# A hybrid decoder step: earlier conditioning weights, convolution taps by channel block, and eight weight slots for the experts

## The reference, cut to what matters

```python
def ada_mod(c, w, b):                       # 9 conditioning rows, w is 1024 x 6144 per layer
    return jnp.split(jax.nn.silu(c) @ w + b, 6, axis=-1)

# layer 0: attention beside a Conformer convolution
q, k, v, ga, gb = jnp.split(h @ w_in, ...)  # 5 blocks of 512 columns
q = rmsnorm(q, q_gain); k = rmsnorm(k, k_gain)           # by heads of 64
u = ga * jax.nn.sigmoid(gb)
cv, new_buf = causal_dwconv(u, conv_buf, cb_w)           # 31 taps, 512 channels
cv = jax.nn.silu(layernorm(cv + cb_b, cb_ln_g, cb_ln_b))
out = jnp.concatenate([o, cv], axis=-1) @ w_out

# layer 1: a short gated convolution; after each: a mixture of 32 experts
g_idx = argmax(xf @ w_group + b_group)                   # 1 of 4 groups
top_v, top_i = lax.top_k(e_in_group, 2)                  # 2 of its 8 experts
y_e = (jax.nn.silu(x @ gate[e]) * (x @ up[e])) @ down[e] # 1024 -> 2*512 -> 1024
```

## Time and profile before

| what | value |
|---|---|
| runs of the kernel before (three) | 2438.08, 2447.42, 2448.91 us; median 2447.42 |
| the profiled execution | 2444.9 us, its span 2443.2 us |
| PE busy | 1804.6 us (74%) in matmuls |
| DVE, ACT, POOL busy | 487.0, 300.4, 179.7 us |
| data moved | 604.27 MB, mean 247 GB/s |
| granted TensorE clock, mean | 0.863 of full speed |

### The profile page before, as it was taken

One profiled execution on the slowest core, in us unless ns is written; L12 is line 12 of the kernel. 1 busy time (PEld: TensorE's weight loads), 2 busy tenths in 40 slices (PEclk: granted clock), 3 DMA queues, 4 the chain that ended last, 5 costly groups with the idle time before them and its releaser, 6 DMA issues. The chain is left out here.

```text
span 2443.2 us, 26085 instructions
## 1 busy us (share of the span) xinstructions
PE 1804.6 (74%) x8637; PEld 846.2 (35%) x8638; DVE 487.0 (20%) x989; ACT 300.4 (12%) x563; POOL 179.7 (7%) x167
## 2 busy tenths in 40 slices
PE   3779877368867478888888718999944788787682
PEld 1335333134433333333333204555442333332231
DVE  0010695332132201100000031121131010000003
ACT  1130111322101010010101012000020101010001
POOL 0000111001102200000000030000121000000004
PEclk8769989568688589999999968999967999899896
DMA  7992203907701277799999990010045999999994
GB/s 252 387 383 72 69 18 104 351 30 238 285 22 69 91 301 272 297 407 410 408 411 411 410 342 2 1 69 2 35 172 215 354 366 411 409 411 411 411 410 174
DMA packets 194115, 604.27 MB, mean 247 GB/s; under 512 B 15951, under 2 KB 18288, under 8 KB 193897
## 3 DMA queue, kind: packets, MB, share of 16 engines
q1 hardware_dynamic: 158064, 522.21, 55.1%
q10 hardware_dynamic: 25761, 46.50, 5.2%
q0 software_dynamic: 10208, 34.48, 4.0%
HBM read 551.57 MB, written 52.01 MB: 247 GB/s over the span
## 5 line engine op out<-in xcount | busy, mean ns | idle before, releaser
L780 PE MATMUL ps<-ring,W 128*64 128x512 f32 x2048 | 465.4, 605 | 55.5 <-issue 32.7
L793 PE MATMUL ps<-ring,W 128*64 128x512 f32 x1024 | 272.8, 680 | 52.0 <-DVE W L1591 47.2
L780 PEld LDWEIGHTS ps<-ring,W 128*64 128x64 f32 x2048 | 173.2, 139 | 335.7 <-issue 334.9
L909 ACT ACTIVATE W<-ps 128x512 f32<-128x512 f32 (+4 forms) x243 | 134.5, 568 | 973.5 <-PE ps L793 364.3
L1585 DVE TENSOR_TENSOR W<-W,ps 128x256 f32<-128x256 f32 x64 | 26.9, 421 | 796.4 <-ACT W L1175 796.4
L886 PE MATMUL ps<-hT,ring 128*128 128x512 f32 x384 | 170.7, 597 | 0.5 <-DVE W L1609 0.5
L793 PEld LDWEIGHTS ps<-ring,W 128*64 128x64 f32 x1024 | 91.0, 155 | 193.3 <-issue 193.3
L545 PE MATMUL ps<-ring,hT 128*128 128x512 f32 (+1 forms) x240 | 116.9, 646 | 1.9 <-DVE W L1292 1.9
L467 PE MATMUL ps<-ring,cT 128*32 128x512 f32 x384 | 75.8, 931 | 31.9 <-DMA ring<-in_w_ada_dram 31.7
L886 PEld LDWEIGHTS ps<-hT,ring 128*128 128x128 f32 x384 | 71.1, 190 | 80.9 <-issue 80.4
L1304 DVE SCALAR_TENSOR_TENSOR W<-W,prm 128x512 f32<-128x512 f32 x120 | 89.5, 817 | 0.0
(11 more groups left out here) (280 smaller groups left out, 1553.4 us busy)
## 6 DMA issues: line engine op xcount, KB each, us to landing
ring<-in_w_gate_up_dram SPq DMA_DIRECT2D x128, 2048.0 KB, 16.8
ring<-in_w_down_dram SPq DMA_DIRECT2D x64, 2048.0 KB, 17.0
ring<-in_w_ada_dram SPq DMA_DIRECT2D x24, 2048.0 KB, 19.7
x_rows<-X ACTq DMA_DIRECT2D x1, 18944.0 KB, 53.0
ring<-in_cache_k_dram SPq DMA_DIRECT2D x64, 256.0 KB, 3.0
W<-x_rows SPq DMA_DIRECT2D x32, 512.0 KB, 17.8
x_rows<-W ACTq DMA_DIRECT2D x128, 128.0 KB, 5.9
ring<-in_cache_v_dram POOLq DMA_DIRECT2D x48, 256.0 KB, 4.6
```

The lines of the kernel that those rows point to most:

```text
L780: x = mm(ps[CAP * z:CAP * z + CAP, 2 + j, :], xt[:, k, :], at[:, :, 256 * z:256 * z + 256], start=(k == 0), stop=(k == KD - 1))
L793: x = mm(ps[CAP * z:CAP * z + CAP, 5 + j, :], ht[:, k % 2, CAP * (k // 2):CAP * (k // 2) + CAP], ring[:, 3 * j + 2, at:at + 512], start=(k ...
L909: return fn(out, src, ACT.Copy, **k)
```

## The change

Three parts are made together.

1. **Start.** PE adds to `slot_free` as its first act. ACT's transfers get semaphores of their own: `c_in` (c and the constants), `params_in` (nine), `misc_in` (gains of q and k, lambda). ACT computes `silu(c)` after three transfers, and issues `x_prompt` behind that. The eight router transfers move from ACT's queue to SP's, behind the first slot of `w_out_a`.
2. **Convolution.** Taps run by channel block, one block after the other: even taps sum in `cv`, odd taps in the block of `V` not yet in use, and one addition joins them (128 steps in all). 18 steps stand behind each of the first three u steps, and 8 in each q or k turn. ACT waits for the last steps before it writes `V`. The state's load goes to the `raw` area.
3. **Experts.** The ring gets slots 6 and 7, which are `Hb` and `hT` when the router has used them. The 96 loads of a layer go round the eight slots in order, so that a load waits for the part eight loads before. `each_expert` is one loop of four turns over eight experts. A pair of rows beyond the last is fetched and turned too (17 pairs instead of 16), and further passes' rows start 128 later.

```diff
-PAIRS = E // 2
+PAIRS = E // 2 + 1
+NRING = 8
+LOADS = 3 * E // NRING
+        slots = [ring[:, s, :] for s in range(NSLOT)] + [hflat[:, 0:SLOT], tflat[:, 0:SLOT]]
+        steps = [(c, k) for c in range(4) for k in range(BW + 1)]
+        WITH_U, WITH_QK = 18, 8
         def each_expert(eng, step):
-...
+            with eng.Fori(0, E // 8) as r:
+                for i in range(8):
+                    p, q = 4 * r + i // 2, i // 2 + 1
+                    step(8 * r + i, i, r, p, i // 2 % 2, (q % 2, 2 * r + q // 2, 4 * r + q) if i % 2 else None)
+        def place(i, k):
+            return divmod(3 * i + k, NRING)
...
@@ sync
+            for l in range(2):
+                for dst, src in ((rb[:, l, 0:G], a["b_group"][l:l + 1, :].to_broadcast([P, G])),
...
+                    sp.dma_start(dst, src).then_inc(S["route_in"], 16)
...
+                def fetch(r, i, parts=(0, 1, 2)):
+                    for k in parts:
+                        before, part_before = divmod(3 * i + k - NRING, 3)
+                        sp.wait_ge(M[("g0_mm", "gu_mm", "down_mm")[part_before]], done(l, 8 * r + before))
+                        part(EG * (i % 4) + 2 * r + i // 4, k, place(i, k)[1])
+                        if k == 1 and i % 2 == 0:
+                            rows_in(4 * r + (i // 2 + 1), (i // 2 + 1) % 2)
                 layer_wait(sp, l, "disp", 32 * NT)
                 rows_in(0, 0)
                 rows_in(1, 1)
+                layer_wait(sp, l, "lg_mm", 1)
+                part(2 * EG, 0, 6)
+                part(2 * EG, 1, 7)
+                rows_in(2, 0)
+                fetch(0, 2, (2,))
+                for i in range(3, 8):
+                    fetch(0, i)
+                with sp.Fori(1, E // 8) as r:
+                    for i in range(8):
+                        fetch(r, i)
@@ tensor
+            for s in range(NSLOT):
+                pe.sem_inc(slot_free[s], 1)
...
-            pe.wait_ge(S["params_in"], 16 * 26)
+            pe.wait_ge(S["c_in"], 48)
@@ scalar
+            act.wait_ge(S["c_in"], 48)
+            fn(W[0:9, W_C:W_C + D], W[0:9, W_C:W_C + D], ACT.Silu).then_inc(S["c_ev"], 1)
 ...
...
+                if u == 2 * NT:
+                    act.wait_ge(S["conv"], conv_done(2, BW))
@@ vector
+            def conv_step(n):
+                c, k = steps[n]
+                if k == 0:
+                    dve.wait_ge(S["u_ok"], 2 * c + 2)
+                to = V[:, c if c < 3 else LS, :] if k % 2 else cv[:, c, 0:TP]
+                if k >= 2:
+                    dve.wait_ge(S["conv"], n - (1 if k < BW else 0))
...
+                if m < 3:
+                    for n in range(WITH_U * m, WITH_U * (m + 1)):
+                        conv_step(n)
...
-                for n in range(per * u, min(per * u + per, 4 * BW)):
-                    conv_tap(n)
+                for n in range(3 * WITH_U + WITH_QK * u, min(3 * WITH_U + WITH_QK * (u + 1), len(steps))):
+                    conv_step(n)
```

More of the change, by code:

```diff
@@ L213, in mod @@
             return modT[:, MODS * KD * l + KD * m:MODS * KD * l + KD * m + KD, :]
-        slot_in = [sem(f"slot_in{s}") for s in range(NSLOT)]
+        slot_in = [sem(f"slot_in{s}") for s in range(NRING)]
         v_in = [sem(f"v_in{j}") for j in range(2)]
@@ L357, in experts, with part @@
                 dn = a["w_down"][l].rearrange("e (k p) n -> e p k n", p=P)
[L359 removed]
+                def part(e, k, s):
                     src = gu[e, :, 4 * k:4 * k + 4, :] if k < 2 else dn[e, :, :, :]
[L361 to L362 removed]
+                    sp.dma_start(slots[s].rearrange("p (k n) -> p k n", k=4), src).then_inc(slot_in[s], 16)
                 for s in range(NSLOT):
@@ L392, in experts @@
                 rows_in(1, 1)
[L393 to L409, removed]
+                layer_wait(sp, l, "lg_mm", 1)
[8 more added lines that the diff above has]
+                        fetch(r, i)
             experts(0)
             winc = a["w_in_c"][0].rearrange("(k p) n -> p k n", p=P)
-            for j in range(2):
-                for k in slots_done(0, E - 2 + j):
-                    col = D * k + 512 * j
-                    load(3 * j + k, winc[:, :, col:col + 512])
+            for s in range(NSLOT):
+                last, part_last = divmod(3 * E - NRING + s, 3)
+                sp.wait_ge(M[("g0_mm", "gu_mm", "down_mm")[part_last]], done(0, last))
+                col = D * (s % 3) + 512 * (s // 3)
+                load(s, winc[:, :, col:col + 512])
             woutc = a["w_out_c"][0].rearrange("(k p) n -> p k n", p=P)
@@ L457, in _ @@
             pe.sem_inc(S["row_tr"], 2)
-            for s in range(NSLOT):
-                pe.sem_inc(slot_free[s], 1)
+            pe.wait_ge(S["params_in"], 16 * 9)
+            tr(ps[:, 6, 0:96], W[0:96, 0:P], ident[0:96, 0:96])
+            tr(ps[:, 6, 96:165], W[0:69, P:2 * P], ident[0:69, 0:69])
+            tr(ps[:, 6, 165:289], W[0:124, 2 * P:3 * P], ident[0:124, 0:124]).then_inc(S["prm_tr"], 1)
             with pe.Fori(0, 4) as it:
@@ L774, in ffn, with gate_up @@
                 layer_wait(pe, l, "gate2_ev", 4)
-                def gate_up(xt, j, half, signal):
+                def gate_up(xt, i, half, signal):
+                    j, slot = i % 2, slots[place(i, half)[1]]
                     for k in range(4 * half, 4 * half + 4):
-                        at = ring[:, 3 * j + half, D * (k % 4):D * (k % 4) + D].rearrange("p (g f) -> p g f", g=2)
+                        at = slot[:, D * (k % 4):D * (k % 4) + D].rearrange("p (g f) -> p g f", g=2)
                         for z in range(2):
@@ L787, in h_turns, with down @@
                     x.then_inc(signal, 1)
-                def down(ht, j, signal):
+                def down(ht, i, signal):
+                    j, slot = i % 2, slots[place(i, 2)[1]]
                     for k in range(FE // P):
@@ L837, in one_pass @@
                                 x = mm(ps[XC * z:XC * z + XC, 5 + j, 0:256], hhT2[:, k, :],
-                                       ring[:, 3 * j + 2, at:at + 256], start=(k == 0), stop=(k == 3))
+                                       slots[place(i, 2)[1]][:, at:at + 256], start=(k == 0), stop=(k == 3))
                         x.then_inc(F["products"], 1)
```

167 lines of the change are left out of this document (78 added, 89 removed).

## The result

The changed kernel takes **2487.2 us** (median of 4, 2477 to 2509) where the kernel before takes 2446.6: the ratio is 1.018, with a 95% interval of 1.011 to 1.026. It is slower; forecast were 2417 us. The profiled execution took 2494.8 us with a span of 2493.0, 49.8 us more than the span of before, 2443.2.

A forecast was written before the change was run, and what follows sets the result against it. Transfers were taken to bound the start, DVE's taps the convolution, and PE, with loop code fetched anew, the experts. 2444.9 - 19 - 33 + 24 = 2417 us, range 2372 to 2446.

The forecast's parts named there:

- Part 1: Start, `w_ada` stage: first weight load at about 1 us instead of 28.38, gain 19 us, bounds 12 and 27.
- ACT's late entry: Start: ACT enters its loop near 28 us, behind the lambda transfers, at little cost; at 35 us in the lower bound.
- Part 2: Taps' stage: a turn on DVE falls from 11.52 to 7.8 us, nine intervals, gain 33 us.
- The rival by which the two-deep chain waits for itself: Taps on DVE: steps cost 0.9 us, a turn 9.0, gain only 22, total 2428 us; no chance of its own given.
- Part 3: Experts: more PE time for new loop code outweighs the ring's lead; layer 0 +18, layer 1 +6, together +24 us.
- the price of the code of the loop: Experts' loop: twelve packets do not stay; nine more misses at 4.1 us, 37 us of PE per layer.
- the price of a table load: Experts, ACT's silu table: 2.9 us per load, three fewer loads give back 9 us per layer.
- the third load ahead: Experts' start, a sign: SP issues three weight loads between rows and first freed slot; the working said two loads ahead.
- The mean price of an ordinary late step: Experts, PE on new code: mean idle 2.85 us per late step, besides +1.3 for the dearer product.
- a sign of a slower kernel: Experts: more than one step in three starting late would mean slower; about one in four was expected.
- The upper bound of +57: Experts, part 3's upper bound: 5.5 us a miss and no table load saved, 45 us per layer.
- The slower rival: Experts: a miss at every branch over the passes' code, +220 us, 2613 us; over 2460 us had chance 0.08.

The follow-up runs named there:

- experiment 1: The changed start and taps on the kernel before, with its experts (six slots, loop of four steps) untouched: 2396.9 us, ratio 0.981.
- Experiment 8: The changed kernel with PE's 32 expert steps written out and the other engines' loops untouched: 2437.5 us, ratio 0.995 to the kernel before.
- experiment 4: The changed kernel with six slots, four steps in the loop and 93 never-executed PE products added per step: 2817.7 us, ratio 1.152 to the kernel before.
- experiments 3 to 7 and 12: Changed kernel with six slots: eight steps (2489.1 us), or four steps plus 93, 24, 38, 54, 12 never-executed products per step (2817.7, 2635, 2715, 2714, 2433 and 2484).

## Why the prediction was wrong

- **Part 1: right.** Forecast were 19 us from a load at 1 us; the norm's transposes, which follow the stage, start at 158.04 instead of 176.80, 18.8 us. ACT's late entry came at 33.5 us, in the bounds given, and cost nothing, since the transfers and not PE set the stage's end.
- **Part 2: right.** Forecast 33 us, measured 31.3 (50.1 us ahead at 360.83, less 18.8). The turn is 8.1 us for 7.8. The rival by which the two-deep chain waits for itself, 0.9 us a step, fell: eight steps take 6.39 us, 0.80 each, though that is a little over the 0.747 of the forecast.
- **Between them and the experts** 3.5 us were lost. Profiled executions of nearly the same code take 444.0 us (experiment 1), 450.7 (before) and 454.2 (changed) from the barrier behind the taps to the first gate-up product, so I give this no cause.
- **Part 3: the step that failed**, the price of the code of the loop. Right were that twelve packets do not stay, that the passes' code and not the ring matters, that PE would wait for no weight (12 us given back in layer 0 and 26 in layer 1; forecast 10 and 22), and that silu's table is loaded eight times. Wrong was the price of a table load, 2.9 us: PE's waits for DVE shrank by 3 and 5.5 us per layer, forecast 9. The two steps compared, 15.86 and 12.92 us, differ in more than the load: the second turns a pair of rows, during which silu is made, and its down products take 3.65 us where the first's take 5.35. The next step of the first's kind without a load, 2040.74 to 2055.21 in the trace of before, takes 14.47 us, which makes 1.4 us a load and 4 for three. Also wrong, but of no weight, was the third load ahead: there are two, as the working itself said.

The sum of part 3 was to be +24 us and is +56.9 and +42.4, 99 us. Its terms in layer 0, forecast against measured (the measured ones over 815 to 1431 of the changed kernel and 861 to 1421 of the kernel before; PE was busy for 454.17 us there):

| term, layer 0 | forecast | measured |
|---|---|---|
| three branches back, pause | 3 x 2.85 = 8.6 | 29.6 |
| other late steps, pause, less those of before | 6 x 2.85 = 17 | 30.3 - 7.2 = 23.1 |
| products dearer (lower granted clock) | 9 x 1.3 = 12 | 472.37 - 454.17 = 18.2 |
| fewer table loads (waits for DVE) | -9 | -3 |
| waits for weights given back | -10 | -12 |
| sum | +18 | +56 |

Of the 18.2 us, 1.1 are the turn of the added pair of rows. PE's waits for DVE of all kinds were 73.3 us before and are 70.5; the largest part, ahead of the turns of h, in us, number and longest, before and after:

```profile
PE ps L786 <- DVE W L1585: 29.9, 24, 2.5
```

```profile
PE ps L797 <- DVE W L1613: 24.3, 20, 2.5
```

The mean price of an ordinary late step was right: 30.3 / 10 = 3.0 us for 2.85. There were more of them (ten, not eight; thirteen in layer 1); with the branches back 13 and 16 of 32 steps came late, over one in three, which the prediction had named as a sign of a slower kernel. But the large item is the first: over both layers the six branches back are 57.9 us of pause where 17.1 were forecast, 41 of the 75 us that the sum of part 3 missed. I had priced a branch back to code that is no longer held like a late step in straight code, because the earlier trace rows had only such; no row of the kernel before shows a branch back that misses. That is an unknown cost, and I bounded it by the nearest row without asking what is different behind a branch back. Experiment 8 shows the size, 50 us for six of them. Why a packet costs less in straight code no run here shows. The upper bound of +57, 5.5 us a miss, was too low for the same reason, and the chance of 0.08 for over 2460 us was what came.

The slower rival named the right engine and the right threshold (it was to decide from 42 us of PE per layer on; layer 0 lost 57, layer 1 42) but the wrong mechanism, a miss at every branch over the passes' code; that would have given 32 late steps per layer, and there were 13 and 16, three of them dear. With loops longer by dead code (experiment 4) it begins to be true.

## What to carry to other kernels

Before a loop is unrolled, count the code of the engine that bounds it, the parts that are jumped over included, and compare it with a length that the trace shows to stay; here a loop of 5.9 packets of PE cost nothing, one of 6.7 was on the edge and one of 7.5 or more paid 9 to 12 us at every branch back. Look at the other engines' loops too: when PE's pauses were gone in experiment 8, ACT's came to light. A cost of which the trace holds no example is not bounded by its mildest relative. Where several edits go together, time the sum without each: two of these three were worth 47 us, and the third took 90.

## What the chip showed that I had not expected

- A branch back to code of PE that is no longer held costs 9.0 to 12.1 us of pause (seen in experiments 3 to 7 and 12 and in the changed kernel), some three times what a late packet in straight code costs (up to 3.6 us in experiment 8), and the gate-up product behind it took 8.5 to 10.1 us, where 7.07 is the rule.
- The limit is sharp and lies below eight packets: 2398 us at 5.9 packets, 2433 to 2484 at 6.7, 2635 at 7.5.
- Code that is never executed cost up to 420 us, where the kernel without it takes 2398.
- ACT too came late at its branches back in the loop of eight steps. It showed only in experiment 8, where PE had no such pause: PE then waited up to 7.2 us for the product with silu, against 2.5 in the changed kernel.
